# The head of a two-block program: shift and scale columns in pairs, the first normed input and the first three units' products inside the first block, and three low parts on GpSimd

## The reference, cut to what matters

```
c_act = silu(c)
mod = c_act @ w_ada[l] + b_ada[l]
shift1, scale1, gate1, shift2, scale2, gate2 = split(mod, 6)
h = rms_norm(x, norm1_g[l]) * (1.0 + scale1) + shift1
z = h @ w_in[l]
```

## Time and profile before

| | |
|---|---|
| median of 3 runs | 2464.11 us (2463.63 to 2464.44) |
| profiled execution | 2463.14 us |
| its span in the trace | 2461.3 us |
| TensorE busy, of the span | 96% |
| VectorE busy | 73% |
| ScalarE busy | 47% |
| GpSimd busy | 6% (148.3 us) |
| first block, until the next one's first transfer is issued | 38.18 us |

### The profile page before, as it was taken

One profiled execution on the slowest core, in us unless ns is written; L12 is line 12 of the kernel. 1 busy time (PEld: TensorE's weight loads), 2 busy tenths in 40 slices (PEclk: granted clock), 3 DMA queues, 4 the chain that ended last, 5 costly groups with the idle time before them and its releaser, 6 DMA issues. The chain is left out here.

```text
span 2461.3 us, 36638 instructions
## 1 busy us (share of the span) xinstructions
PE 2364.9 (96%) x14280; PEld 2123.6 (86%) x14280; DVE 1797.1 (73%) x2913; ACT 1157.5 (47%) x1707; POOL 148.3 (6%) x141
## 2 busy tenths in 40 slices
PE   4979999999999999999999999999999999999998
PEld 4879898888888888889899888888888888898998
DVE  7979997677667676678999676566767576555665
ACT  4542255444545454564135444455545523544554
POOL 0000153000000000000045100000000000000000
PEclk9989999999999999999999999999999999999999
DMA  9365544787676666434544586665555523343553
GB/s 356 134 227 163 157 124 149 267 298 240 233 242 231 239 231 223 148 111 139 177 135 125 188 299 220 204 216 187 189 188 191 191 78 108 124 148 126 189 186 107
DMA packets 133554, 460.63 MB, mean 187 GB/s; under 512 B 15152, under 2 KB 16432, under 8 KB 132912
## 3 DMA queue, kind: packets, MB, share of 16 engines
q1 hardware_dynamic: 133424, 458.90, 55.1%
HBM read 445.73 MB, written 13.11 MB: 186 GB/s over the span
## 5 line engine op out<-in xcount | busy, mean ns | idle before, releaser
L1654 DVE TENSOR_TENSOR ring_lo<-ring,ring_hi 128x1024 fp32r<-128x1024 f32 x421 | 506.9, 1222 | 88.6 <-ACT ring_hi L1557 88.6
L1557 ACT ACTIVATE ring_hi<-ring 128x1024 fp32r<-128x1024 f32 x421 | 435.0, 1054 | 134.0 <-PE banks L346 119.9
L319 PE MATMUL banks<-normed_lo,ring_hi 128*128 128x512 f32 x1344 | 477.9, 398 | 0.0
L344 PE MATMUL banks<-ring_hi,work_lo 128*128 128x512 f32 x1024 | 400.5, 391 | 8.0 <-DVE work_lo L1681 4.3
L345 PE MATMUL banks<-ring_lo,work_lo 128*128 128x512 f32 x1024 | 399.9, 391 | 0.0
L346 PE MATMUL banks<-ring_hi,work_lo 128*128 128x512 f32 x1024 | 399.1, 390 | 0.0
L320 PE MATMUL banks<-normed_lo,ring_lo 128*128 128x256 f32 x1344 | 377.2, 281 | 0.0
L319 PEld LDWEIGHTS banks<-normed_lo,ring_hi 128*128 128x128 f32 x1344 | 252.5, 188 | 61.8
L361 DVE TENSOR_TENSOR ring_lo<-ring,ring_hi 128x1024 fp32r<-128x1024 f32 x185 | 225.0, 1222 | 78.1 <-ACT ring_hi L356 77.5
L320 PEld LDWEIGHTS banks<-normed_lo,ring_lo 128*128 128x128 f32 x1344 | 253.8, 189 | 3.3
L1677 DVE TENSOR_TENSOR work<-banks,work 128x512 f32<-128x512 f32 x84 | 58.1, 692 | 249.2 <-ACT work L1563 249.2
(11 more groups left out here) (387 smaller groups left out, 4357.4 us busy)
## 6 DMA issues: line engine op xcount, KB each, us to landing
ring<-wstream SPq DMA_DIRECT2D x716, 512.0 KB, 3.3
arena<-wstream SPq DMA_DIRECT2D x96, 512.0 KB, 5.7
spill<-one_hots SPq DMA_DIRECT2D x44, 256.0 KB, 4.2
rstd<-spill SPq DMA_DIRECT2D x16, 256.0 KB, 4.1
pool_and_keys<-spill SPq DMA_DIRECT2D x14, 256.0 KB, 4.1
routes<-spill SPq DMA_DIRECT2D x14, 256.0 KB, 4.8
residual<-xT SPq DMA_DIRECT2D x1, 1024.0 KB, 7.8
arena<-mixconst SPq DMA_DIRECT2D x2, 512.0 KB, 4.2
```

What stands on the lines that cost most here:

```text
L319: pe.matmul(dst, w_hi[:, o], HR[:, k, :], start=(k == 0), stop=(k == KD - 1), skip_group_check=True)
L344: pe.matmul(dst, hi[:, t], w_hi[:, o], start=first, stop=False)
L1557: sc.activation(RING_HI[:, u % HIGHS, :], RING[:, u % SLOTS, :], ACT.Copy)\
L1654: dve.tensor_tensor(RING_LO[:, u % SLOTS, :], RING[:, u % SLOTS, :], RING_HI[:, u % HIGHS, :].bitcast(F32), ALU.subtract).then_inc(S("spli ...
```

## The change

In the first block:

- **Transfers.** The two vector transfers go right behind the c row. Weights come in pairs k and k + 8 (shift and scale of chunk k): pair 0 before the constants, pair 1 behind X, then ring units 0 to 2, pairs 2 to 7, ring units 3 to 7. The copy of the c row moves into layer 0's block, behind late column 11.
- **Columns.** `tensor_tensor_reduce` starts its sum at the b_ada column instead of 0. Behind each pair one small `tensor_scalar` makes the gain of that chunk. The three operations at the block's end go.
- **Normed input.** `flow_scaled` and `flow_low` are called one by one between the pairs, and `high_flow` runs at the end of ScalarE's part.
- **Low parts of ring units 0 to 2** are made by GpSimd; their high parts move forward on ScalarE (two before the root, one behind).
- **Products of units 0 to 2** are made at the end of TensorE's part, chunk by chunk, after GpSimd's three low parts.

In layer 0's block `high_flow`, `norm_flow` and that `unit_group` go; layer 1 keeps them.

```
 SyncE, first block
                 sp.dma_start(CROW, crow).then_inc(S("c_row"), 16)
-                ada(0, 2)
+                for layer in range(DEPTH):
+                    sp.dma_start(LVS[:, layer, :], wstream[layer * PER_LAYER + U_PARAMS][:, 0:L_COLS])\
+                        .then_inc(S(f"vectors{layer}"), 16)
+                pair(0)
                 (constants, positions, X)
-                (the two vectors) 
-                ada(2, 11)
-                sp.wait_ge(S("c_act"), 1)
-                sp.dma_start(CROW_KEPT, CROW).then_inc(S("c_row_kept"), 16)
+                pair(1)
                 ring(0, PRE)
-                ada(11, N_ADA)
+                for k in range(2, KD):
+                    pair(k)
                 ring(PRE, SLOTS)
 TensorE, first block, at the end
+                pe.wait_ge(S("first_low"), PRE)
+                unit_group(pe, range(PRE), [PS[:, 2 + i, 0:T] for i in range(PRE)], (True,) * PRE)
 GpSimd, first block
+                for u in range(PRE):
+                    pool.wait_ge(S("high"), u + 1)
+                    pool.tensor_tensor(RING_LO[:, u, :], RING[:, u, :], RING_HI[:, u, :].bitcast(F32), ALU.subtract)\
+                        .then_inc(S("first_low"), 1)
 ScalarE, first block
+                for u in range(PRE - 1):
+                    split_high(act, u, True)
                 token_root(act)
+                split_high(act, PRE - 1, True)
                 (the two tables)
-                for u in range(PRE):
-                    split_high(act, u, True)
+                high_flow(act, H, MOD[:, 0:8])
 VectorE, first block
+                def modulate(i):
+                    v.wait(f"ada{i}", 16)
+                    v.mark(dve.tensor_tensor_reduce(ADA[i], ADA[i], CROW, 1.0, col(LV, L_BADA + i), ALU.mult, ALU.add,
+                                                    MOD[:, i:i + 1]), "modulated")
+                def pair(k):
+                    modulate(k)
+                    modulate(k + KD)
+                    v.wait("modulated", 2 * k + 2)
+                    v.mark(dve.tensor_scalar(S1G[:, k:k + 1], MOD[:, KD + k:KD + k + 1], 1.0, col(LV, L_N1 + k),
+                                             ALU.add, ALU.mult), "gain")
+                def scaled(k):
+                    v.wait("gain", k + 1)
+                    flow_scaled(v, H, S1G[:, 0:8], k)
+                pair(0); the angles; pair(1); pair(2); token_inverse(v); pair(3)
+                v.wait("rstd_spread", 1)
+                scaled(0); scaled(1); low 0
+                pair(4); scaled(2); low 1
+                pair(5); scaled(3); low 2; scaled(4); low 3
+                pair(6); scaled(5); low 4
+                pair(7); scaled(6); low 5; scaled(7); low 6; low 7
 layer's block
                 SyncE, behind late_units(9, 12):
+                    if layer == 0:
+                        sp.dma_start(CROW_KEPT, CROW).then_inc(S("c_row_kept"), 16)
                 TensorE, ScalarE, VectorE:
+                    if layer:
                         unit_group(...) / high_flow(...) / norm_flow(...)
```

More of the change, by code:

```diff
@@ L529, in ring @@
                         sp.dma_start(RING[:, u, :], wstream[STREAM[u]]).then_inc(loaded[u], 16)
+                def pair(k):
+                    ada(k, k + 1)
+                    ada(k + KD, k + KD + 1)
                 sp.dma_start(CROW, crow).then_inc(S("c_row"), 16)
-                ada(0, 2)
+                for layer in range(DEPTH):
+                    sp.dma_start(LVS[:, layer, :], wstream[layer * PER_LAYER + U_PARAMS][:, 0:L_COLS])\
+                        .then_inc(S(f"vectors{layer}"), 16)
+                pair(0)
                 sp.dma_start(CST[:, :], consts).then_inc(S("consts"), 16)
@@ L535, in _ @@
                 sp.dma_start(X[:, :, :], xT).then_inc(S("x_loaded"), 16)
-                for layer in range(DEPTH):
-                    sp.dma_start(LVS[:, layer, :], wstream[layer * PER_LAYER + U_PARAMS][:, 0:L_COLS])\
-                        .then_inc(S(f"vectors{layer}"), 16)
-                ada(2, 11)
-                sp.wait_ge(S("c_act"), 1)
-                sp.dma_start(CROW_KEPT, CROW).then_inc(S("c_row_kept"), 16)
+                pair(1)
                 ring(0, PRE)
-                ada(11, N_ADA)
+                for k in range(2, KD):
+                    pair(k)
                 ring(PRE, SLOTS)
-                sp.wait_ge(S("c_row_kept"), 16)
                 for layer in range(DEPTH):
@@ L554, in _ @@
                 spread_rstd(pe)
+                pe.wait_ge(S("first_low"), PRE)
+                unit_group(pe, range(PRE), [PS[:, 2 + i, 0:T] for i in range(PRE)], (True,) * PRE)
+            @block.gpsimd
+            def _(pool):
+                for u in range(PRE):
+                    pool.wait_ge(S("high"), u + 1)
+                    pool.tensor_tensor(RING_LO[:, u, :], RING[:, u, :], RING_HI[:, u, :].bitcast(F32), ALU.subtract)\
+                        .then_inc(S("first_low"), 1)
             @block.scalar
@@ L576, in _, with pair @@
                 v.mark(dve.memset(EPS_COL, EPS), "eps")
[L578 to L585, removed]
+                LV = LVS[:, 0, :]
+                def modulate(i):
+                    v.wait(f"ada{i}", 16)
+                    v.mark(dve.tensor_tensor_reduce(ADA[i], ADA[i], CROW, 1.0, col(LV, L_BADA + i), ALU.mult, ALU.add,
+                                                    MOD[:, i:i + 1]), "modulated")
+                def pair(k):
+                    modulate(k)
[6 more added lines that the diff above has]
+                    flow_scaled(v, H, S1G[:, 0:8], k)
+                v.wait("vectors0", 16)
+                v.wait("c_act", 1)
+                pair(0)
                 v.wait("positions", 16)
@@ L591, in _ @@
                 quarter_turn(v, red2, red, tmp)
-                ada(2, 6)
+                pair(1)
+                pair(2)
                 token_inverse(v)
[L594 to L603, removed]
-                v.wait("rstd_spread", 1)
-                v.wait("split", PRE)
+                pair(3)
+                v.wait("rstd_spread", 1)
+                scaled(0)
+                scaled(1)
+                flow_low(v, H, MOD[:, 0:8], 0)
+                pair(4)
+                scaled(2)
+                flow_low(v, H, MOD[:, 0:8], 1)
+                pair(5)
+                scaled(3)
+                flow_low(v, H, MOD[:, 0:8], 2)
+                scaled(4)
+                flow_low(v, H, MOD[:, 0:8], 3)
+                pair(6)
+                scaled(5)
+                flow_low(v, H, MOD[:, 0:8], 4)
+                pair(7)
+                scaled(6)
+                flow_low(v, H, MOD[:, 0:8], 5)
+                scaled(7)
+                flow_low(v, H, MOD[:, 0:8], 6)
+                flow_low(v, H, MOD[:, 0:8], 7)
         end_of_block()
@@ L673, in _ @@
                         late_units(12 + 3 * i // 2, 12 + 3 * (i + 1) // 2)
+                    if layer == 0:
+                        sp.wait_ge(S("c_row_kept"), 16)
                 @block.gpsimd
@@ L775, in mix_pool @@
                         mm.then_inc(S("pool_mixed"), 1)
-                    unit_group(pe, range(S_IN, S_IN + PRE), [PS[:, 2 + i, 0:T] for i in range(PRE)], (True,) * PRE)
+                    if layer:
+                        unit_group(pe, range(S_IN, S_IN + PRE), [PS[:, 2 + i, 0:T] for i in range(PRE)], (True,) * PRE)
                     unit(3)
@@ L853, in _ @@
                     act = Steps(sc, S)
-                    high_flow(act, H, MOD[:, 0:8])
+                    if layer:
+                        high_flow(act, H, MOD[:, 0:8])
                     def next_high(i):
@@ L972, in modulation @@
                                                             MOD[:, 16 + k:17 + k]), "modulated")
-                    norm_flow(v, H, S1G[:, 0:8], MOD[:, 0:8])
+                    if layer:
+                        norm_flow(v, H, S1G[:, 0:8], MOD[:, 0:8])
                     def low(i):
```

## The result

The changed kernel takes 2473.79 us (median of 6 runs, 2470.25 to 2477.05), the kernel before 2463.87 (6 runs): ratio 1.0041, 95% interval 1.0028 to 1.0054, so 9.9 us slower; 2472 had been forecast, range 2464 to 2477. Beside another set of runs of before it measured 1.0037 (1.0023 to 1.0051).

A forecast was written before the change was run, and what follows sets the result against it. VectorE was taken to bound the layer from 55 us on; unit 4's low part moves +8.5, less the rotation's wait +8.0: 2463.14 + 8.0 = 2471.1, with the runs' median 0.97 above the profiled time 2472, range 2464 to 2477.

The forecast's parts named there:

- The critical place: Unit 4's low part on VectorE, at 52.74 before, behind four late columns whose fourth waits for its transfer until 51.59.
- Exclusion: Head, columns 2 and 10: GpSimd's low parts and VectorE's column products exclude each other for whole operations, costing 3.8 us.
- Rival A: Head: column products run free beside GpSimd, so everything is 3.8 us earlier, 2468.3; chance 0.20.
- Pairs and chunks: Head, VectorE: column 2 taken at 20.2, columns 1.15 each, pairs 2.6, chunks 0.40; last low chunk done at 46.9.
- Products in the head: TensorE's 27 matmuls of chunks 5 to 7 end at 49.9, between 48.6 fast and 51.2 slow; block starts at 50.4.
- Late columns laid bare: Layer 0's block: first late column lands at +5.1, fourth at +9.6; unit 4's low part at +10.8, 61.2.
- The rest: Behind unit 4's low part: the rotation's 0.48 wait at 54.78 goes, so +8.5 becomes +8.0 us from there.
- rival C: Units 3 and 4: TensorE comes cold, 2.3 to 4.6 us on top, 2474.5 to 2479; 0.14 shared with another rival.
- Rival B: Unit 3's products: TensorE, not the fourth late column, sets the pace; +2.4 us, 2466.5; chance 0.15.

The follow-up runs named there:

- Experiment 3: Changed kernel with the weights of late columns 0 to 2 issued at the end of the first block; ratio to before 1.0019.
- experiment 1: Changed kernel with the three low parts back on VectorE and GpSimd idle in the head; ratio to before 1.0024.
- experiment 2: Changed kernel with low parts back on VectorE and GpSimd writing 16 memsets to unused memory; ratio to before 1.0023.
- experiment 4: Changed kernel with low parts back on VectorE and late columns 0 to 2 issued early; ratio to before 1.0011.
- experiment 5: Changed kernel with the 72 products of units 0 to 2 back at the start of layer 0's block; ratio to before 1.0025.
- Kernel 6: Kernel before with four buffers for late columns instead of three; ratio to before 0.9999.
- experiment 10: Changed kernel unaltered, timed once more beside the kernel before; ratio to before 1.0037.
- experiment 9: Changed kernel with low parts on VectorE, late columns 0 to 2 issued early and the 72 products back in layer 0's block; ratio to before 1.0033.

## Why the prediction was right, step by step

- *The critical place* was right: VectorE's work between the block's start and the low part of unit 4, with the transfers of the late columns. Experiment 3 issues just those transfers early and gets 4.0 at the rotation.
- *Exclusion*: 3.8 forecast. In the trace the two products end at 27.5 (21.26 to 24.22, and 3.28 to the read at 27.50). Alone, with column 10 landing 1.25 after column 2, they would have ended at 22.5 + 1.2 = 23.7. That is 3.8. GpSimd's operations were 2.31 apart, not 2.2. Rival A falls, with experiments 1 and 2. The trace agrees with the Trainium skill here (SBUF — State Buffer, Who interferes with whom), which says that a VectorE instruction with two SBUF inputs contends with a GpSimd instruction that reads SBUF and not with one that only writes it: 3.03 and 3.35 us beside GpSimd's subtractions, 1.26 to 1.29 beside its memsets.
- *Pairs and chunks*: column 2 could be taken at 21.26, not 20.2, as transfers landed later; a column whose sum starts from the b_ada column took 1.20 in sequence, not 1.15; last low chunk at 48.1 where 46.9 was forecast.
- *Products in the head*: these 1.2 us did not reach the block's start, since TensorE was already at its upper level (0.120) for all of chunks 5 to 7, for which the middle between the two levels had been taken. The last matmul ended at 50.16 (49.9 forecast), the block started at 50.45 (50.4). Two errors cancel here; the step was right only in its sum.
- *Late columns laid bare* is the term that was mis-sized: late column 0 landed 6.1 after the block's start, not 5.1, and the low part of unit 4 came at +12.0, not +10.8. From there the forecast is 1.2 low: 62.45 against 61.2.
- *The rest*: +9.1 at the first rotation (8.0 forecast); 0.8 more at the rotation at 74.66, after unit 4 had run at a granted clock of 0.50. That is a part of what rival C priced, 0.8 and not 2.3 to 4.6. The wait is 0.69 in the changed kernel run again, and 0.49 and 0.42 in kernels 1 and 2, where unit 4 ran at a granted clock of 0.50 too; kernels 3, 4 and 5, where it ran at 1.00, have no such wait.
- *The distance behind the head*. At 74.66 it is 10.1 (64.61 in before), and 10.1 again at 169.29. It stays so up to a transfer issued at 432.55 (422.43 in before). The next one, 442.28 against 430.26, is 12.0 behind: between them the granted clock reads 0.50 (435 to 438), and 1.00 in before. Kernel 6, which was level with before until there, has such a stretch too (0.50 from 425 to 427), so it doesn't take the changed head. The span's further distance, up to 12.6, thus comes from where the granted clock fell in that execution. The head's part is 10.1 here and 9.2 in experiment 10, and the medians say 9.9 and 9.1 us in time.
- *Rival C's upper end* is mis-added: 2472 + 4.6 is 2476.6, not 2479, so the range up to 2477 left out nothing of it.
- *Rival B*, TensorE sets the pace, does not hold for the changed kernel (experiments 3 and 5), but does for one step further (experiment 9), and in the kernel before both engines are within a microsecond of each other (experiment 6). The forecast argued from VectorE alone there and was lucky in that the change hurt VectorE by far more than TensorE.

What the change meant to gain was taken from TensorE's side of a tie; it paid on VectorE's side: 3.8 to exclusion and 4.0 to late transfers that the moved work had hidden. Without these two losses (experiment 4) it is level with before at 169.29 (+0.1), 2.7 us above it in time, and in neither faster.

## What to carry to other kernels

Work moved out of a block takes with it the cover that it gave to transfers issued at the block's start: move the transfers too, or price them as if nothing ran. An operation given to GpSimd is not free for VectorE as such: here three subtractions that read the on-chip memory held its two-input products up by 3.8 us, and memsets did not. Look for the slowest instance of such an operation in the trace, not the mean. And where one engine's time is taken off a path, look first for the other engine that reaches the same point within a microsecond, since it takes the gain back. A pause that a change opens on TensorE has a price of its own where it is followed by work that others wait for: read the granted clock in narrow stretches behind the pause, as a mean over a long one hides it.

## What was not expected of the hardware

- TensorE's spacing of 0.120 survived gaps of 0.31 and 2.12 us in the changed kernel's head, and was lost over gaps of 3.05 and 4.45. The same gap of 2.12 ended at the lower level in kernel 1 (granted clock 0.50), so the length of a gap alone does not tell.
- The granted clock read 1.00 while the first products of a kernel went at a spacing of 0.213 (up to 43.5 in before, 42.3 in the changed kernel); later on the same spacing went with a reading of 0.50.
- A column product whose sum starts from a column in memory instead of the constant 0 was recorded at 1.28 us instead of 1.22, and came 1.20 after the one before instead of 1.15.
- GpSimd's subtraction of 128x1024 took 2.34 us without VectorE in its way, 3.32 with a product in front of it; the two engines took turns operation by operation, though GpSimd's were queued back to back.
